# Ten query and key chunks of the second block as five pairs a layer, each by seven block products

## The reference, cut to what matters

```python
h = rmsnorm(x, g_norm)
z = jnp.einsum('bsd,dn->bsn', h, w_in)
dq, dk, dv, dg, lq, lk, lv, lg, mq, mg, mgate = jnp.split(z, splits, axis=-1)
o_a = diff_attention(dq, dk, dv, lam, rel_bias)   # 8 heads, two maps each
outs = [dilated_group(lq[:, :, g], lk[:, :, g], lv[:, :, g], ...) for g in range(3)]
o_m = memory_attention(mq, mk, mv)
...
return x + jnp.einsum('bsd,de->bse', merged, w_out)
```

## Time and profile before

| | |
|---|---|
| median of three runs | 2078.16 us (2077.25 to 2079.62) |
| span of the profiled execution | 2078.3 us; no other time of that execution is shown |
| first block | about the first 1118 us of the span |
| second block, layer 0 and layer 1 | from about 1130 and 1600 us of the span |
| busy share of the span | TensorE 88%, VectorE 36%, ScalarE 19%, GpSimd 6% |

### The profile page before, as it was taken

How to read it: one execution, slowest core, us unless ns; L and a number is a source line. 1 busy time by engine, 2 the same in 40 slices (tenths; PEclk the granted TensorE clock), 3 DMA queues, 4 the chain that set the end, 5 groups by cost and what they waited for, 6 DMA issues and landing times.

```text
span 2078.3 us, 35046 instructions
## 1 busy us (share of the span) xinstructions
PE 1822.0 (88%) x15030; PEld 1208.6 (58%) x15030; DVE 756.2 (36%) x1288; ACT 385.1 (19%) x889; POOL 127.6 (6%) x186
## 2 busy tenths in 40 slices
PE   8998776777699877766769999999999999999998
PEld 4756455455557555554554588746554588746553
DVE  5651111111144111111105503473757503474656
ACT  4511011011022101100112112222221112222121
POOL 1200000000000000000001401200221001200000
PEclk9999988988899989889989999999999999999999
DMA  8599999999999999999998863443646563443331
GB/s 334 177 365 415 419 421 420 420 420 420 420 397 378 420 420 421 420 420 420 420 419 311 178 202 129 135 162 122 172 154 210 118 206 127 137 153 130 132 122 61
DMA packets 155639, 588.62 MB, mean 283 GB/s; under 512 B 16468, under 2 KB 34260, under 8 KB 106456
## 3 DMA queue, kind: packets, MB, share of 16 engines
q1 hardware_dynamic: 146936, 567.45, 70.9%
q0 software_dynamic: 8544, 18.89, 3.7%
HBM read 577.90 MB, written 8.39 MB: 282 GB/s over the span
## 4 chain that ended last, share of the span: by engine, by line
PE 62%; DMA 17%; SPq 12%; DVE 6%; issue 2%; ACT 1%; DVEq 0%; ACTq 0%
PE ps L640 17%; DMA ring<-in_moe_w_dram 16%; PE ps L607 15%; SPq L1397 8%; PE ps L1677 5%; SPq L1406 4%; PE ps L1657 3%; PE ps L1712 3%; PE ps L613 2%; PE ps L584 1%; PE ps L1968 1%; PE ps L617 1%; PE ps L523 1%; PE ps L557 1%; PE ps L1732 1%
## 5 line engine op out<-in xcount | busy, mean ns | idle before, releaser
L1677 PE MATMUL ps<-ring,xT 128*32 128x128 f32 x8192 | 302.8, 306 | 177.9 <-DMA ring<-in_moe_w_dram 171.9
L1677 PEld LDWEIGHTS ps<-ring,xT 128*32 128x32 f32 x8192 | 262.9, 121 | 243.7 <-DMA ring<-in_moe_w_dram 186.1
L607 PE MATMUL ps<-xT,ring 128*128 128x256 f32 x1408 | 310.1, 380 | 0.0
L607 PEld LDWEIGHTS ps<-xT,ring 128*128 128x128 f32 x1408 | 265.3, 190 | 39.7 <-issue 4.9
L2394 DVE TENSOR_TENSOR arena<-arena,ps 128x256 f32<-128x256 f32 x32 | 13.5, 421 | 558.3 <-ACT arena L2062 558.3
L1089 DVE TENSOR_TENSOR ring<-ring 128x2048 f32<-128x2048 f32 x64 | 146.7, 2292 | 15.6 <-PE ps L640 6.9
L640 PE MATMUL ps<-ring,xT 128*128 128x512 f32 x336 | 151.1, 594 | 0.5 <-ACT xT L774 0.5
L1712 PE MATMUL ps<-arena 128*32 128x512 f32 x768 | 120.1, 607 | 31.6 <-DVE arena L2394 31.6
L1330 POOL DMA_DIRECT2D ring<-gap_bias x160 | 96.4, 672 | 796.9 <-DMA ring<-in_w_in_dram 475.4
L1657 PE MATMUL ps<-arena,x_tm 128*128 128x128 f32 x1024 | 137.3, 291 | 0.0
L1657 PEld LDWEIGHTS ps<-arena,x_tm 128*128 128x128 f32 x1024 | 128.9, 205 | 10.8 <-issue 10.7
(11 more groups left out here) (316 smaller groups left out, 2003.0 us busy)
## 6 DMA issues: line engine op xcount, KB each, us to landing
ring<-in_moe_w_dram SPq DMA_DIRECT2D x287, 1024.0 KB, 26.1
arena<-in_moe_w_dram SPq DMA_DIRECT2D x89, 1024.0 KB, 26.8
ring<-in_w_in_dram SPq DMA_DIRECT2D x44, 2048.0 KB, 8.5
ring<-in_w_in_dram SPq DMA_DIRECT2D x16, 1024.0 KB, 12.1
ring<-in_w_br_diff_dram SPq DMA_DIRECT2D x4, 2048.0 KB, 10.5
ring<-in_w_out_dram SPq DMA_DIRECT2D x4, 2048.0 KB, 8.0
arena<-in_moe_w_dram SPq DMA_DIRECT2D x14, 512.0 KB, 15.6
ring<-in_w_mem_kv_dram SPq DMA_DIRECT2D x3, 2048.0 KB, 18.9
```

The source lines that it names most:

```text
L607: m = nc.tensor.matmul(bank[:, u * T:(u + 1) * T], w[:, k, f * P:(f + 1) * P], xT[:, k, :], start=(k == 0), stop=(k == KD - 1))
L1677: m = nc.tensor.matmul(ps[SL * q:SL * q + SL, g % 2, s * P:(s + 1) * P], xs[:, g % 2, k, s * SL:(s + 1) * SL], w[:, c0:c0 + 2 * P - 1:2], ...
```

## The change

Chunks 0 and 1, 2 and 3, 8 and 9, 10 and 11, 12 and 13 become pairs (plan indices 4, 6, 8, 10 and 12), in both layers. Pairs 4 and 6 have no head beside them; 8, 10 and 12 have two differential heads each. Their products keep the layout by feature: the weights stay the stationary operand, and 128 tokens move in place of 256. A product is four feature blocks of four matmuls. The outputs go to `dqk` and `lqk` through views of 128 columns. The scores of head 0 now wait for VectorE's fourth output of pair 6. ScalarE squares the second head of a pair ahead of the pair's last copy. The generic `product` and `take` lose these chunks.

```diff
+BY_FEATURE = (0, 2, 8, 10, 12)
 PAIRS = [i for i, (c, _, _) in enumerate(PLAN)
-         if c == ("br_diff", 0) or (c[0] == "w_in" and c[1] in (4, 6, 14, 16, 20, 22, 24))]
+         if c == ("br_diff", 0) or (c[0] == "w_in" and c[1] in BY_FEATURE + (4, 6, 14, 16, 20, 22, 24))]
...
+        def as_taken(i, bank):
+
+            return bank.rearrange("p (f t) -> p f t", f=CW // P) if by_feature(i) else bank
...
+        def pair_outs(l, i, n):
+
+            return 4 * (l * (len(PAIRS) - 1) + PAIRS.index(i) - 1) + n
+
         def pair_outputs(i):
 
             c = PLAN[i][0][1]
+            if by_feature(i):
+                dst, f0 = (dqk, 4 * c) if c < 4 else (lqk, 4 * (c - 8))
+                return [dst[:, f0 + 4 * cc:f0 + 4 * cc + 4, t * P:(t + 1) * P] for t in range(TT) for cc in range(2)]
...
                 if h == 0:
                     wait_taken(pe, l, last)
+                    if kind == "diff":
+                        pe.wait_ge(sem("pair_out"), pair_outs(l, chunk_of("w_in", 2), 4))
...
                 (a11, a12, _, a22), (s1, s2, s3, _) = x_blocks(i), x_combined(i)
+                if by_feature(i):
+                    w = (wa[:, :KH], wb[:, KH:], wa[:, KH:], wa[:, :KH], wb[:, KH:], wa[:, KH:], wb[:, :KH])[u]
+                    for f in range(CW // P):
+                        for k in range(KH):
+                            x_ = S4_of[k] if u == 1 else (a11, None, a12, s1, s2, a22, s3)[u][:, k, :]
+                            m = nc.tensor.matmul(ps[:, bank_at(l, n), f * P:(f + 1) * P], w[:, k, f * P:(f + 1) * P],
+                                                 x_, start=(k == 0), stop=(k == KH - 1))
+                    m.then_inc(sem("bank_full"), 1)
+                    return
...
-                nc.scalar.copy(dst, ps[:, bank_at(l, n), :]).then_inc(taken_of(l, n), 1)
+                nc.scalar.copy(dst, as_taken(i, ps[:, bank_at(l, n), :])).then_inc(taken_of(l, n), 1)
...
                     take_turned([PT3[:, m, :] for m in range(TURNS[job1[0]])])
+                if job1 and job1[0] == "diff":
+                    square_head(l, job1[1], job_n + 1)
...
-                    ch(nc.vector.tensor_tensor(dst, first_parts[i], ps[:, bank_at(l, n), :], ALU.add))
+                    ch(nc.vector.tensor_tensor(dst, first_parts[i], as_taken(i, ps[:, bank_at(l, n), :]), ALU.add))
```

More of the change, by code:

```diff
@@ L327, in build, with by_feature @@
         KH, COMBINED, TANHS = KD // 2, len(COMBOS), 20
+        def by_feature(i):
+            (name, c), _, _ = PLAN[i]
+            return name == "w_in" and c in BY_FEATURE
+        def as_taken(i, bank):
+            return bank.rearrange("p (f t) -> p f t", f=CW // P) if by_feature(i) else bank
         S1, S2, S3x = consts[:, P:P + KH * P], gap_rows[:, :], x_comb[:, 0:KH * P]
         S4_of = [arena[:, AW - 3 * P + k * P:AW - 2 * P + k * P] for k in range(3)] + [x_comb[:, KH * P:]]
-        first_parts = {i: PT3[:, 0, :] if i == GATE else S3[:, 2, :] for i in PAIRS}
+        first_parts = {i: as_taken(i, PT3[:, 0, :] if i == GATE else S3[:, 2, :]) for i in PAIRS}
         S_dil = S3[:, 0:2, :].rearrange("p m k -> p (m k)").rearrange("p (t k) -> p t k", t=TT)
@@ L602, in product @@
                 w = cslots[s]
-                if by_feature(name, c):
+                if name == "w_in" and c == 18:
                     for u in range(2):
@@ L752, in pe_second @@
                 assert turned[0] == 2 + (l + 1) * NTURN - (0 if l + 1 < DEPTH else 2) and job_n == NJOB
-        def by_feature(name, c):
-            return name == "w_in" and (c < 4 or 8 <= c < 14 or c == 18)
         def squares(act, l, t):
@@ L809, in take @@
                 taken = taken_of(l, n)
[L810 to L815, removed]
+                if c == 18:
                     nc.scalar.copy(mqT[:, 2 * half:2 * half + 2, :], two).then_inc(taken, 1)
@@ L822, in copy_product @@
                 act.wait_ge(sem("bank_full"), filled(l, n + 1))
-                nc.scalar.copy(dst, ps[:, bank_at(l, n), :]).then_inc(taken_of(l, n), 1)
+                nc.scalar.copy(dst, as_taken(i, ps[:, bank_at(l, n), :])).then_inc(taken_of(l, n), 1)
             def pair_tanh(l, i, j, which):
                 c = PLAN[i][0][1]
-                act.wait_ge(sem("pair_out"), 4 * (l * (len(PAIRS) - 1) + PAIRS.index(i) - 1) + j + 1)
+                act.wait_ge(sem("pair_out"), pair_outs(l, i, j + 1))
                 part = pair_outputs(i)[which]
```

## The result

The changed kernel takes 2106.67 us (median of 4 runs, 2103.66 to 2107.54) against 2078.18 of the kernel before: a ratio of 1.0134, 95% interval [1.0122, 1.0146]. It was forecast slower, at 2105, in a range of 2089 to 2112.

What follows compares the result with a forecast made beforehand. The prediction took TensorE as the bound, with VectorE as cover. Two layers of -1.3 + 6.8 + 0.6 + 6.6 + 0.8 gave +27.0 us on 2078.2, forecast 2105 us, range 2089 to 2112.

Steps and rivals of the forecast that it cites:

- TensorE's own saving: Matmuls of a pair: 3.56 us a product, 24.9 a pair against 27.70 for two chunks, 2.8 saved.
- The second head's turn: Pairs beside two heads: TensorE idles 5.2 us (pair 8: 4.2) for VectorE's weighing; +6.8 us a layer.
- The clock: Behind the waits at second heads' turns: clock falls to half, losing 2.3 or 2.0 us each, 6.6 a layer.
- The rival without the fall: Same waits of TensorE, but the clock does not fall: +12.2 us, 2090.4; chance 0.14.
- The plain pairs: Pairs 4 and 6, no heads beside them: 54.8 us against 56.09, -1.3 a layer.
- The second chunk's wait: Pair 4's second product waits 2.4 us for chunk 5's load; half of 1.65 us taken for the clock.
- the wait of head 0's scores: After pair 6, scores wait for VectorE's four blocks, coming at +2.6 us; a slow stretch behind is absorbed by pair 8's idle time.
- Pair 14: Behind the pairs with heads: it starts with a VectorE tail, its turn at +8.65 instead of +8.03 us; +0.6.
- The rival in which VectorE keeps up: Pairs with heads: VectorE on time at the second head's turn, TensorE stays the bound; -18.2 us, 2060; chance 0.06.

Runs made afterwards that it cites:

- The shortened combination: Changed kernel with the fourth combination of the six pairs beside heads made on a quarter of its columns: 2094.92 us, a single run.
- the late turn: Changed kernel with product 5 ahead of the second head's turn and product 6 ahead of its values, ScalarE's copy and VectorE's gate reordered to fit: 2078.38 us.
- filling the waits: Changed kernel with eight idle fp32 matmuls on TensorE ahead of the second head's turn in the six pairs: 2098.48 us, ratio 1.0096.
- the corrected order: All ten pairs reordered on three engines; against the first such order, ScalarE copies product 3 before the second head's exponentials and only pair 4 is swapped: 2063.75 us.
- the run with plain pairs alone: Changed kernel with only chunks 0 to 3 as pairs (indices 4 and 6), chunks 8 to 13 one by one again: 2082.43 us, ratio 1.0015.
- the orders put together: Changed kernel with product 2 before 1 in plain pairs, head 0's scores and second heads' turns later, VectorE's combination and addition earlier: 2086.09 us, ratio 1.0037.

## Why the prediction was right

- **TensorE's own saving** (3.56 a product): measured 3.57 and 3.67, the latter behind another kind of matmul. Writing in pieces of 128 columns cost nothing that shows.
- **The second head's turn** (idle 5.2, start at +27.0): it started at +27.11 in pair 10 (1782.88 behind 1755.77), VectorE's line being right to 0.1. The idle time was 4.9, because TensorE's own line was 0.4 longer. The shortened combination showed the one-for-one dependence, and the late turn that nothing else stood behind it. Pair 8 waited 3.8 for a predicted 4.2 in layer 1; in layer 0 only 3.1, since a slow stretch at its start had held TensorE back. The prediction had that stretch absorbed by the idle time; it was only in part, and pair 8 took 36.73 us in layer 0 for 35.85 in layer 1.
- **The clock** (2.0 to 2.3 a wait): it fell behind all six. Product 5 and the turn lost 1.6 to 2.2 each by the timeline, 11.5 in all, and filling the waits gave back 8.2 to 11.3; the term said 13.2. The rival without the fall was put at 2090.4, and the run without it behind these six waits took 2098.5: the clock's term was a few microseconds too large and the rest as much too small, which was luck for the sum. The rule of the Trainium skill ("TensorE: Matmul & The Clock Gate", section "HAM oscillation — how this bites in real kernels"), that recurring waits bring the half clock back each time, held in this trace for all six.
- **The plain pairs** (-1.3 a layer): -2.0 in layer 1 and +1.7 in layer 0. The second chunk's wait was 0.94 and 3.04 us, for a predicted 2.4 in both. Layer 1 did not stand for layer 0 here; in layer 0 the clock fell behind the longer wait, and again behind the wait of head 0's scores (2.7 us in both layers, predicted 2.6).
- **Pair 14** (+0.6): +0.9 in both layers.

Together: layer 1 +11.8 and layer 0 +16.4 by the windows and the starts of the scores, where 13.5 each was said. The sum was right partly because an error in each layer offset the other's.

The rival in which VectorE keeps up named the right place. That its number is near the corrected order's (2060 said, 2063.75 measured) is luck: it had 8.4 us a layer from the pairs with heads and 1.3 from the plain pairs, where the corrected order has 2.4 and 6.1 in layer 1. What decides it is the order in three queues, not a faster combination, which is where I put its point.

## What to carry to other kernels

When work moves to an engine that looks idle, lay its instructions end to end in program order up to each point where the bound engine waits; the busy share says nothing about which of them comes last. A late wait is often cured by what stands behind it in the waiting engine's queue: work that does not depend on it can go first. And every moved step has to be followed through all queues, the copies that free a bank among them.

## What the runs showed of the hardware that was not expected

A wait of 2.7 us ahead of head 0's scores was followed by a fall of the clock in some runs and layers and not in others, at the same place: in the changed kernel in layer 0 and not in layer 1. Two waits of 0.94 and 1.78 us with 0.7 us of work between them brought the same fall as one long wait in three of four places, while single waits of 1.49 (the shortened combination) and of 1.70 to 1.81 (the orders put together) did not. The price varies as well: the slow stretch behind a wait of 2.7 us lasted 6.7 us in the run with plain pairs alone, where it cost 3.0 us:

```profile
1706.10:1712.80 6.70, 6.09 (x18) 4.56 (x19) 3.57 (x8) 1.84 (x7) 0.00 (x0) 0.50 1.03 384
```

The load of pair 4's second chunk came 2.1 us later against its need in layer 0 than in layer 1. By the trace of the changed kernel it was issued 6.0 us ahead of the pair in layer 0 and 7.7 in layer 1, behind an issue that took 6.36 us on SP's queue in the one and 4.76 in the other, and landed 12.8 and 12.4 us later. Why that issue took longer is open.
